# Two passes in one: the first half of the activation's split beside the second, for seven of the query and key chunks

## The reference, cut to what matters

```
z = rms_norm(x, g_norm) @ w_in
qa, ka, va, ga, fa, qb, kb, vb, gb = split(z)      # the gated heads take qa and ka
c = cumsum(log_sigmoid(fa + b_f))
s = qa . ka * hd**-0.5 + c[q] - c[k]
...
z = rms_norm(x, g_norm) @ w_in                      # the retention layer
q, k, v, g = split(z)
q, k = rotate(q), rotate(k) * 256**-0.5
```

## Time and profile before

| | |
|---|---|
| median of 3 runs | 770.98 us |
| the profiled execution | 770.69 us |
| its span, first to last instruction | 768.9 us |
| around the span | 1.8 us |
| TensorE's granted clock, mean | 0.999 |
| PE / DVE / ACT / POOL busy | 760.5 / 517.2 / 409.8 / 223.6 us |
| channel chunks `qa`, `ka` | 51.97 to 98.05 us of the span |
| channel chunks `rq` 1, `rk` 0, `rk` 1 | 293.45 to 328.05 us of the span |

### The profile page before, as it was taken

How to read it: one execution, slowest core, us unless ns; L and a number is a source line. 1 busy time by engine, 2 the same in 40 slices (tenths; PEclk the granted TensorE clock), 3 DMA queues, 4 the chain that set the end, 5 groups by cost and what they waited for, 6 DMA issues and landing times.

```text
span 768.9 us, 12573 instructions
## 1 busy us (share of the span) xinstructions
PE 760.5 (99%) x5026; PEld 658.3 (86%) x5026; DVE 517.2 (67%) x779; ACT 409.8 (53%) x664; POOL 223.6 (29%) x176
## 2 busy tenths in 40 slices
PE   9999999999999999999999999999999999999997
PEld 8889987899877899987778888988888888888885
DVE  5876756665577558765567965778788676667553
ACT  6674458443696453353344554727857555456451
POOL 2110996730940000064029900126012111011010
PEclk9999999999999999999999999999999999999999
DMA  9999893588512746555435565430465556655751
GB/s 284 220 233 301 245 248 65 131 174 198 156 62 80 242 138 194 186 169 159 142 110 164 191 218 168 140 134 30 164 193 152 183 175 204 194 179 175 242 169 55
DMA packets 78490, 132.01 MB, mean 172 GB/s; under 512 B 4592, under 2 KB 28304, under 8 KB 78304
## 3 DMA queue, kind: packets, MB, share of 16 engines
q1 hardware_dynamic: 76928, 126.01, 55.7%
q0 software_dynamic: 1216, 5.09, 2.3%
q10 hardware_dynamic: 288, 0.11, 0.1%
HBM read 130.12 MB, written 1.06 MB: 171 GB/s over the span
## 4 chain that ended last, share of the span: by engine, by line
PE 97%; DVE 1%; ACT 1%; issue 0%; DVEq 0%; ACTq 0%
PE ps L1711 15%; PE ps L1715 15%; PE ps L1719 15%; PE ps L1769 10%; PE ps L1752 6%; PE ps L1756 6%; PE ps L1748 6%; PE ps L1777 5%; PE ps L1839 2%; PE ps L1855 2%; PE ps L1870 2%; PE ps L2225 1%; PE ps L2102 1%; PE ps L2054 1%; PE ps L2110 1%; PE ps L1799 1%
## 5 line engine op out<-in xcount | busy, mean ns | idle before, releaser
L1032 DVE TENSOR_TENSOR w_lo<-stage,w_hi 128x1024 fp32r<-128x1024 f32 x224 | 293.4, 1332 | 150.9 <-ACT w_hi L667 150.2
L667 ACT ACTIVATE w_hi<-stage 128x1024 fp32r<-128x1024 f32 x230 | 239.1, 1060 | 234.1 <-PE ps L1719 104.8
L1711 PE MATMUL ps<-w_hi,act_t 128*128 128x512 f32 (+1 forms) x368 | 100.5, 396 | 0.2 <-ACT act_t L694 0.2
L1719 PE MATMUL ps<-w_lo,act_t 128*128 128x512 f32 (+1 forms) x368 | 96.5, 385 | 0.0
L1769 PE MATMUL ps<-act_t,w_hi 128*128 128x512 f32 x352 | 84.1, 391 | 0.0
L1719 PEld LDWEIGHTS ps<-w_lo,act_t 128*128 128x128 f32 x368 | 68.1, 188 | 14.0
L1711 PEld LDWEIGHTS ps<-w_hi,act_t 128*128 128x128 f32 x368 | 66.5, 188 | 15.1 <-issue 2.5
L1715 PE MATMUL ps<-w_hi,act_t 128*128 128x512 f32 (+1 forms) x304 | 79.4, 384 | 0.0
L1769 PEld LDWEIGHTS ps<-act_t,w_hi 128*128 128x128 f32 x352 | 64.7, 188 | 12.6
L1715 PEld LDWEIGHTS ps<-w_hi,act_t 128*128 128x128 f32 x304 | 56.1, 188 | 11.6
L1748 PE MATMUL ps<-act_t,w_hi 128*128 128x256 f32 x416 | 58.8, 284 | 0.0
(11 more groups left out here) (384 smaller groups left out, 1153.1 us busy)
## 6 DMA issues: line engine op xcount, KB each, us to landing
stage<-in_even_w_in SPq DMA_DIRECT2D x62, 512.0 KB, 5.4
stage<-in_odd_w_in SPq DMA_DIRECT2D x48, 512.0 KB, 3.9
stage<-in_w_gate_up SPq DMA_DIRECT2D x44, 512.0 KB, 4.8
stage<-in_w_down SPq DMA_DIRECT2D x22, 512.0 KB, 4.7
stage<-in_even_w_out SPq DMA_DIRECT2D x16, 512.0 KB, 3.8
stage<-in_odd_w_out SPq DMA_DIRECT2D x16, 512.0 KB, 3.8
stage<-in_w_in SPq DMA_DIRECT2D x10, 512.0 KB, 3.7
stage<-in_w_out SPq DMA_DIRECT2D x8, 512.0 KB, 4.5
```

Source lines behind the costliest of these rows:

```text
L667: nc.scalar.activation(w_hi[:, u % RING, :], stage[:, u % RING, :], ACT.Copy).then_inc(hi_ready, 1)
L1032: nc.vector.tensor_tensor(w_lo[:, u % RING, :], stage[:, u % RING, :], w_hi[:, u % RING, :].bitcast(F32), ALU.subtract).then_inc(lo_ready, 1)
L1711: mm(out[:, b, :], a_hi(k)[:, tok[b]], hi[:, i, :], start=(k == 0), stop=False)
L1719: ins = mm(out[:, b, :], a_hi(k)[:, tok[b]], lo[:, i, :], start=False, stop=(k == k_tiles - 1))
```

## The change

Seven of the eight chunks named above get the form of the feed-forward part: `qa` 0 and 1, `ka` 0 and 1, `rq` 1, `rk` 0 and 1 (`rq` 0, whose activations are still being split while it runs, keeps its three passes). In `wide_channels_unit` a unit is 8 matmuls of 512 columns (upper weights by upper and lower x) and 8 of 256 (lower weights). Each such chunk fills four banks in place of two (`WIDE`), so some waits are new and the lag matrices move from bank 7 to bank 4. ACT copies the second halves in two instructions for each chunk (`take_lower`), and DVE adds the first halves in two more before it goes on; `take_heads` and the rotation then read the sums from SBUF in place of PSUM.

```diff
--- before.py
+++ after.py
@@ -291,6 +291,7 @@
         prob_copied, prob_copied_act = sem("prob_copied"), sem("prob_copied_act")
         inv_ready, gate_scaled, gate_copied, heads_out = sem("inv_ready"), sem("gate_scaled"), sem("gate_copied"), sem("heads_out")
         wave_ready, wave_sin = sem("wave_ready"), sem("wave_sin")
+        lower_out, parts_added = sem("lower_out"), sem("parts_added")
         ret_scores, ret_decayed, ret_pv, ret_var, ret_scale, ret_centered, ret_out = (sem(n) for n in ("ret_scores", "ret_decayed", "ret_pv", "ret_var", "ret_scale", "ret_centered", "ret_out"))
         drive_done, drive_read, v_ready, scan_done, state_ready, y_done = (sem(n) for n in ("drive_done", "drive_read", "v_ready", "scan_done", "state_ready", "y_done"))
         b_pow_ready, c_pow_ready, lag_done, lag_copied, lag_ready, fade_ready = (sem(n) for n in ("b_pow_ready", "c_pow_ready", "lag_done", "lag_copied", "lag_ready", "fade_ready"))
@@ -318,6 +319,16 @@
 
         def ffn_turned_at(k):
             return (4, 2, 5, 3)[k] * BANK if k < 4 else 4 * BANK + k * S
+
+        WIDE = {("qa", 0): (0, 1, 2, 3), ("qa", 1): (4, 5, 6, 7), ("ka", 0): (0, 1, 2, 3), ("ka", 1): (4, 5, 6, 7),
+                ("rq", 1): (2, 3, 6, 7), ("rk", 0): (0, 1, 4, 5), ("rk", 1): (2, 3, 6, 7)}
+        wide_names = list(WIDE)
+
+        def wide_parts(name, pair):
+
+            at = WIDE[name][2 * pair] * BANK
+            both = ps[:, at:at + 2 * BANK].rearrange("p (m v n) -> p m v n", m=2, v=2)
+            return both[:, :, 0, :], both[:, :, 1, :]
 
         def chunk_done(eng, name):
 
@@ -805,6 +816,17 @@
                 act.wait_ge(prob_turned, n + 1)
                 nc.scalar.activation(prob_slots[:, n % SLOTS, :], bank(turned_at(n), 384), ACT.Copy).then_inc(prob_copied_act, 1)
 
+            def take_lower(name, dst):
+
+                ahead(name)
+                chunk_done(act, name)
+                for pair in range(2):
+                    nc.scalar.activation(dst[pair], wide_parts(name, pair)[1], ACT.Copy).then_inc(lower_out, 1)
+
+            heads_of_chunk = lambda dst, c: [dst[:, 4 * c + 2 * pair:4 * c + 2 * pair + 2, :] for pair in range(2)]
+            for kind, dst in (("qa", q0), ("ka", k0)):
+                for c in range(2):
+                    take_lower((kind, c), heads_of_chunk(dst, c))
             for half in range(2):
                 v = "va" if half == 0 else "vb"
                 if half == 1:
@@ -852,13 +874,16 @@
             split_hi(chunks[("even_out", 0)][0] + 4)
             hi_of_wide(range(4, 8))
             out_and_turn("even_out", 1, KD + 8, COL_ODD)
-            for kind, n in (("rq", 2), ("rk", 2)):
-                for c in range(n):
-                    ahead((kind, c))
+            for kind, dst in (("rq", q1), ("rk", k1)):
+                for c in range(2):
+                    if (kind, c) in WIDE:
+                        take_lower((kind, c), [dst[:, 2 * c + hh] for hh in range(2)])
+                    else:
+                        ahead((kind, c))
             act.wait_ge(lag_done, 1)
             for q in range(4):
                 r = slice(32 * q, 32 * q + 32)
-                nc.scalar.activation(lag[r, :, :, r].rearrange("p s t n -> p t s n"), ps[r, 7 * BANK:8 * BANK].rearrange("p (t s n) -> p t s n", t=CT, s=STEP),
+                nc.scalar.activation(lag[r, :, :, r].rearrange("p s t n -> p t s n"), ps[r, 4 * BANK:5 * BANK].rearrange("p (t s n) -> p t s n", t=CT, s=STEP),
                                      ACT.Copy).then_inc(lag_copied, 1)
             for c in range(4):
                 ahead(("rv", c))
@@ -1214,6 +1239,16 @@
 
                 row = rstd_row_q if name[0] == "q" else rstd_row
                 ahead((name, c))
+                if (name, c) in WIDE:
+                    out = [dst[:, 4 * c + 2 * pair:4 * c + 2 * pair + 2, :] for pair in range(2)]
+                    for pair in range(2):
+                        dve.wait_ge(lower_out, 2 * wide_names.index((name, c)) + pair + 1)
+                        TT(out[pair], wide_parts((name, c), pair)[0], out[pair], ALU.add).then_inc(parts_added, 1)
+                    for pair in range(2):
+                        dve.wait_ge(parts_added, 2 * wide_names.index((name, c)) + pair + 1)
+                        ins = TT(out[pair], out[pair], row[:].unsqueeze(1).to_broadcast([P, 2, S]), ALU.mult)
+                    ins.then_inc(drain_sem((name, c)), 1)
+                    return
                 chunk_done(dve, (name, c))
                 for pair in range(2):
                     ins = TT(dst[:, 4 * c + 2 * pair:4 * c + 2 * pair + 2, :], result((name, c))[:, pair, :].rearrange("p (m n) -> p m n", m=2),
@@ -1322,11 +1357,19 @@
             for kind, dst in (("rq", q1), ("rk", k1)):
                 for c in range(2):
                     ahead((kind, c))
+                    wide = (kind, c) in WIDE
+                    for hh in range(2):
+                        if wide:
+                            both, count = dst[:, 2 * c + hh], 2 * wide_names.index((kind, c)) + hh + 1
+                            dve.wait_ge(lower_out, count)
+                            TT(both, wide_parts((kind, c), hh)[0], both, ALU.add).then_inc(parts_added, 1)
                     chunk_done(dve, (kind, c))
 
                     for hh in range(2):
                         h = 2 * c + hh
-                        src = result((kind, c))[:, hh, :].rearrange("p (e n) -> p e n", e=2)
+                        if wide:
+                            dve.wait_ge(parts_added, 2 * wide_names.index((kind, c)) + hh + 1)
+                        src = dst[:, h] if wide else result((kind, c))[:, hh, :].rearrange("p (e n) -> p e n", e=2)
                         by_cos = prob_t[:, :, :].rearrange("p a b -> p (a b)")[:, 0:512].rearrange("p (e n) -> p e n", e=2)
                         by_sin = prob[:, :, :].rearrange("p a b -> p (a b)")[:, 512:1024].rearrange("p (e n) -> p e n", e=2)
                         TT(by_cos, src, rot[:, 0, :].unsqueeze(1).to_broadcast([P, 2, S]), ALU.mult)
@@ -1756,6 +1799,23 @@
                         ins = mm(out[m], columns(lo[:, i, :], m), act_t[:, k, :], start=False, stop=(k == k_tiles - 1), skip_group_check=True)
                 ins.then_inc(unit_used, 1)
 
+            def wide_channels_unit(name, j, k_tiles, columns, there=always):
+
+                hi, lo = unit_of(name, j)
+                both = act_t[:, :, :].rearrange("p (v k) n -> p v k n", v=2)
+                ks = range(2 * j, 2 * j + 2)
+                for i, k in enumerate(ks):
+                    there[0](k)
+                    there[1](k)
+                    for m in range(4):
+                        mm(bank(WIDE[name][m]).rearrange("p (v n) -> p v n", v=2), columns(hi[:, i, :], m), both[:, :, k, :], start=(k == 0), stop=False,
+                           skip_group_check=True)
+                lower_there(name, j)
+                for i, k in enumerate(ks):
+                    for m in range(4):
+                        ins = mm(bank(WIDE[name][m], S), columns(lo[:, i, :], m), act_t[:, k, :], start=False, stop=(k == k_tiles - 1), skip_group_check=True)
+                ins.then_inc(unit_used, 1)
+
             def ffn_two_units(name, first, there=always, between=None):
 
                 both = act_t[:, :, :].rearrange("p (v k) n -> p v k n", v=2)
@@ -1789,7 +1849,10 @@
             def channels(name, columns=plain, there=always):
                 start_chunk(name)
                 for j in range(chunks[name][1]):
-                    channels_unit(name, j, KD, columns, there)
+                    if name in WIDE:
+                        wide_channels_unit(name, j, KD, columns, there)
+                    else:
+                        channels_unit(name, j, KD, columns, there)
 
             def after_lo(count):
                 return lambda k: pe.wait_ge(act_hi, count + k + 1), lambda k: pe.wait_ge(act_lo, count + k + 1)
@@ -1825,7 +1888,9 @@
                 mm(bank(4, S), w, x_hi(k), start=(k == 0), stop=False)
                 ins = mm(bank(4, S), w, x_lo(k), start=False, stop=(k == KD - 1))
             ins.then_inc(f_done, 1)
+            chunk_drained(pe, ("ga", 1))
             channels(("qa", 0))
+            pe.wait_ge(f_abs, 1)
             channels(("qa", 1))
 
             for name in (("ka", 0), ("ka", 1)):
@@ -2027,15 +2092,18 @@
                 if j == 3:
                     row_of_diag()
                 channels_unit(("rq", 0), j, KD, pairs, after_lo(KD + 8))
-            for name in (("rq", 1), ("rk", 0), ("rk", 1)):
-                channels(name, pairs)
+            channels(("rq", 1), pairs)
+            pe.wait_ge(row_taken, 2)
+            channels(("rk", 0), pairs)
+            channels(("rk", 1), pairs)
             pe.wait_ge(c_pow_ready, 3)
+            chunk_drained(pe, ("rk", 0))
             for ct in range(CT):
                 for c in range(2):
                     for at in range(2):
```

(4 more changed lines are left out.)

## The result

The kernel after has a median of 773.14 us (772.33 to 777.11, 10 runs) beside 771.16 (770.47 to 771.63, 10 runs) for the kernel before: a ratio of 1.0032, with a 95% interval of 1.0020 to 1.0045. It is slower by 2.0 us. The forecast was 768.3 in a range of 767.4 to 770.3, so both the sign and the range were wrong. Of the matmuls, 224 are gone, as they should be.

What follows compares the result with a forecast made beforehand. TensorE (PE), busy 760.5 of 768.9 us, was taken as the bound. Profiled execution 770.69 less 2.7 saved is 768.0; the median lies 0.3 above, so 768.3 us, range 767.4 to 770.3 (8 in 10).

Steps and rivals of the forecast that it cites:

- The multiplications that follow read SBUF in place of PSUM at the same price.: DVE's multiplications after the additions: no added cost; 691 ns for one in SBUF, read in the feed-forward part.
- I take no wait here: Last unit of `ka` 1, tightest in the gated stretch: lower part ready in time, up to 1 us as other end.
- My dear case for one take: Take of `ka` 0, ahead of `ka` 1's last unit: four slowed DVE operations, 4 us in place of 1.2; just in time.
- Rival 1: `ka` 1: DVE late because POOL's work slows it, 1 us lost, 769.3 us; chance 12%.
- the 1.5 forecast: PE in the gated heads' chunks: 16 units in the wide form save 1.5 us.
- the 1.1 forecast: PE in retention's chunks: 12 units in the wide form save 1.1 us.
- Seven chunks of four units are 28 units: 2.7 us: PE over all changed chunks: 0.095 us saved per unit, 2.7 us in all, bounds 2.5 to 2.9.
- rival 3: Wide matmuls in the changed chunks cost two narrow ones, 240 ns, so nothing is won: 771.0 us; chance 5%.
- the lead at the end of `rq` 1: DVE's lower part for `rk` 0's last unit: lead shrinks from 4.9 to 2.7 us, backlog then worked off.
- rival 4: Retention: DVE falls behind, its 11.0 us per chunk filling 11.1; at 3 us more per chunk 774.6 us; chance 7%.
- Rival 2: Gated stretch bound by transfers: its 1.5 us go, only retention's 1.1 us stay, 769.8 us; chance 8%.
- ACT's copies were free: ACT in the changed chunks: 14 added copies, 8 us in total, 1.1 us per chunk, all beside PE.

Runs made afterwards that it cites:

- e3_sum_in_psum: Kernel after, but the additions write their sum back into PSUM and the gated multiplications read it there: 768.95 us, ratio 0.9971 to the kernel before.
- e10_gpsimd_idle: Kernel after with GpSimd's 12 additions shrunk to 4 columns each and its later work held to the stretch's end (output differs): 768.71 us, ratio 0.9961.
- e7_operand_in_sbuf: Kernel before, but ACT copies the gated chunks' result to SBUF and DVE multiplies it there in place; no additions: 771.00 us, ratio 0.9999.
- e5_broadcast_later: Kernel after, but GpSimd's 2 MB transfer of the forget gate's sums waits for one more weight unit: 771.58 us, ratio 1.0000 to the kernel before.
- e8_psum_x_later: Kernel after with the sum of the halves in PSUM and the load of x moved behind unit 42: 769.10 us, ratio 0.9970 to the kernel before.
- e6_psum_and_loads: Kernel after with the sum in PSUM, the 2 MB transfer behind unit 25 and the load of x behind unit 42: 769.11 us, ratio 0.9974.
- e4_x_later: Kernel after with the loads of x that stand among the weights moved behind the gated stretch: 773.29 us, ratio 1.0034 to the kernel before.
- e1_gated_only: Kernel after with only the four gated chunks wide, retention's three as in the kernel before: 773.74 us, ratio 1.0034 to the kernel before.
- e11_no_additions: Kernel after without the eight gated additions; the multiplications scale ACT's copies (output differs): 772.54 us, ratio 1.0016 to the kernel before.
- e2_retention_only: Kernel after with only retention's three chunks wide, the gated ones as in the kernel before: 770.18 us, ratio 0.9988 to the kernel before.

## Why the prediction was wrong, step by step

**The step that failed** is the cost of the gated multiplications: "The multiplications that follow read SBUF in place of PSUM at the same price." The price is the same in `qa` 0 and in retention, where GpSimd is idle. In the other three gated chunks it is 1.2 to 1.6 us for one in place of 0.6 (2.37 and 3.15 for two against 1.27), because the second operand in SBUF meets GpSimd's work (its additions, and behind them its powers). Reading PSUM again removes it (675 ns, `e3_sum_in_psum`), and so does an idle GpSimd (681 ns, `e10_gpsimd_idle`); the operand alone brings it into the kernel before (1228 ns, `e7_operand_in_sbuf`). What it is worth in time is 4.2 us: 773.14 against 768.95. The price of 691 ns was read in the feed-forward part, where POOL is busy for only 10.40 of 90 us (600 to 690 of the span).

The row that should have warned me was in my hands. The lower parts, which read `stage` and `w_hi` in SBUF, took 7.91 us for four "while POOL is at work", and 1.2 each elsewhere. I took that as a property of the lower parts, where the multiplications show it too as soon as they read SBUF twice, and the edit turned eight of the kernel's instructions into that kind. The Trainium skill (SBUF — State Buffer, "Who interferes with whom") states it: a DVE instruction with two inputs in SBUF contends with a GpSimd instruction that reads SBUF, for a port that they share, the one that comes second is blocked, and a DVE instruction with at most one SBUF input outside the two-port modes is not. By that rule, the additions from PSUM stay at 676 ns, the multiplications rise, and this is what the trace shows. It also lists `tensor_scalar` as able to use both ports, and so to contend. The trace bears that out in part only: `c_both`, one such, takes 1.51 us in the kernel after and 0.42 where it runs before GpSimd starts (`e5_broadcast_later`: 422 ns), but also 0.41 beside GpSimd's additions in `e3_sum_in_psum` (at 84.30), behind a multiplication that reads PSUM. Why it is slow in the one and not in the other stays open.

**"I take no wait here" (`ka` 1's last unit).** Wrong, and `ka` 0's last unit, which I did not look at, was late as well. My dear case for one take, 4 us in place of 1.2, was about right (2.37 + 1.28 = 3.65), but I priced it for that one take alone. From `qa` 1 on it came in three takes and in `c_both`, with no gap in between, and the delays added up: 29.2 us for what takes 23.2 in `e3_sum_in_psum`. **Rival 1** (12%, 769.3) named the right mechanism with a price of 1 us. With the waits that follow it, it is 4.2. Its argument against, that DVE idled 10.2 us for `w_hi`, fell because that idle time lies ahead of 88 us, and idle time before a backlog doesn't pay for it.

**The late weight unit** I had not seen. In the kernel before, DVE took `qa` 1 at 75.20, ahead of GpSimd's additions from 76.57; in the kernel after at 79.52, behind a unit that landed late beside the 2 MB transfer. That the transfer delays it is shown by `e5_broadcast_later`, where it starts behind the unit (at 68.89) and the unit is in time. Why it does so in the wide kernels and not before stays open: the transfer starts 0.8 us sooner in the kernel after (64.91 against 65.68), but in `e3_sum_in_psum` later (66.24), with the unit later still. The late unit costs nothing in `e10_gpsimd_idle` and `e8_psum_x_later`, and one wait of 1.6 us in the profiled execution of `e3_sum_in_psum`; the medians with the operand in PSUM (`e3_sum_in_psum`, `e8_psum_x_later`, `e6_psum_and_loads`) agree within 0.2 us. With the slow multiplications, having it in time is worth 773.14 - 771.58 = 1.6 us. The loads of `x` have no part (`e4_x_later`).

**The wait that followed.** PE's longest wait, 1.92 us at 128.56, is 26 us behind the stretch. ACT's copy of the probabilities stands in its program behind a `w_hi` that waits for a late load, and the loads are late since lower parts that free their buffers were. That chain is read from the trace, not tested by itself; but it is in every kernel in which the multiplications read SBUF beside GpSimd with the wide form (1.9, 0.8, 1.3, 1.6 and 0.6 us in after, `e1_gated_only`, `e4_x_later`, `e5_broadcast_later`, `e11_no_additions`), and in none of the others.

**The saving on PE.** The pace was right: 230 ns and 2.79 us for a unit in the gated chunks. Where nothing stalls (`e8_psum_x_later`), `qa` to `va` takes 44.70 against 46.07 in the kernel before: 1.4 us for the 1.5 forecast. Retention gives 34.74 - 34.09 = 0.65 for the 1.1 forecast: "Seven chunks of four units are 28 units: 2.7 us" used the feed-forward part's pace for weights that are read with a stride of two. The narrow form, which I took as evidence that the stride is free, doesn't show it; the wide one does, 235 ns for 230. That is a part of **rival 3** come true, 5 ns of the 11. Together the two stretches save 2.0. All ten kernels with retention's wide chunks are also about 0.5 us quicker from the lag matrices (their second line, L2112) to the start of the last matmul: 433.99 to 434.13 us, against 434.64 before and 434.48 and 434.50 in `e7_operand_in_sbuf` and `e1_gated_only`. That `e2_retention_only` wins 1.0 us, nearly the 1.1 forecast, is therefore luck: only 0.65 of it is the wide form's. Why the rest is quicker stays open; the bank of the lag matrices is one candidate, and I didn't try it alone.

**What held.** The retention part had no wait: the lead at the end of `rq` 1 was enough, and **rival 4** (DVE behind in retention) didn't occur; that its 774.6 lies near the result is chance. **Rival 2** (transfers take back the gain) would have given 769.8; the gated stretch moves less per us after (0.85 busy against 0.95) and DVE is what PE waits for. ACT's copies were free.

**The best version** is the forecast's own kernel with the sum written to PSUM: `e3_sum_in_psum`, 768.95, 0.29% [0.19, 0.38] below the kernel before, within the range that I had given.

## What to carry to other kernels

An operand that moves from PSUM to SBUF isn't free because its instruction takes as long in a quiet part of the trace: compare it where the other engines are at work, and look whether GpSimd reads SBUF at that time. When an in-order engine is slowed for a while, add up its load over the whole of that while, not over the tightest unit alone; idle time before it counts for nothing. If a sum is made in two steps, leaving the first in PSUM costs nothing here and keeps the second out of the contention.

## What the runs showed of the hardware

- The granted clock can fall to half behind a wait of under 2 us (1.82 in `e1_gated_only`: 1.7 us lost on top), and in other executions it doesn't behind one as long.
- A DVE multiplication of 128 x 512 takes 671 to 679 ns from PSUM and SBUF in the gated stretch, with GpSimd at work or not (means over four, in six kernels), and 674 to 681 from SBUF twice with GpSimd idle (`e10_gpsimd_idle`); from SBUF twice beside GpSimd's work it takes 1165 to 1718 in the mean over `k`'s four (`e4_x_later`, `e11_no_additions`). The loss goes to both sides: GpSimd's own addition takes 1.28 us where DVE is idle (`e8_psum_x_later`, 76.39) and 2.28 beside DVE's lower parts (POOL's timeline of the kernel after, 76.23).
- A wide float32 matmul slows with the stride of its stationary weights where a narrow one doesn't: 235 against 230 ns for 512 columns, 120 for 256 either way.
- A 512 KB unit can land several us late beside a 2 MB transfer (ACT waits 6.70 us for it in the kernel after, 7.61 in `e3_sum_in_psum`). Of itself that cost PE nothing to 1.6 us; beside GpSimd's work it decided how many takes were slow. The kernel with the transfer moved, `e5_broadcast_later`, ran from 768.4 to 774.9 us, a spread whose cause is not shown.
